# One kernel for two transformer blocks: the feed-forward stage's modulation columns computed in wide VectorE sums that TensorE adds up as rows of one PSUM bank

## The reference, cut to what matters

```python
# first block
mod = silu(c) @ w_ada[0] + b_ada[0]                  # 2048 -> 6 * 2048
shift1, scale1, gate1, shift2, scale2, gate2 = split(mod, 6)
h = modulate(rms(x, norm1_w), shift1, scale1)
...                                                   # state space mixer and attention
x = x + gate1 * mixed
h2 = modulate(rms(x, norm2_w), shift2, scale2)
ffn = (silu(h2 @ w_ffn_gate) * (h2 @ w_ffn_up)) @ w_ffn_down     # hidden width 5632
x = x + gate2 * ffn
# second block, layers 0 (attention, also over a context) and 1 (Fourier mixer)
sh_l, sc_l, g_l = split(silu(c_2) @ ada_w_2[i] + ada_b_2[i], 3)      # 2048 -> 3 * 2048
sh_c, sc_c, g_c = split(silu(c_ctx_2) @ ada_w_2[0] + ada_b_2[0], 3)  # layer 0, context
```

## Time and profile before

| | us |
|---|---|
| median of 3 runs | 2577.97 (2577.28 to 2579.29) |
| the profiled execution | 2578.01 |
| its span, first to last instruction | 2576.2 |

### The profile page before, as it was taken

The page is one execution under the profiler, slowest core; times in us unless marked ns, Lnnn a source line. Parts: engine busy times, 40 slices in busy tenths (PEclk is TensorE's granted clock), DMA queues, the critical chain, the costliest instruction groups (busy, mean ns, idle before and its releaser), DMA issues.

```text
span 2576.2 us, 38244 instructions
## 1 busy us (share of the span) xinstructions
PE 2443.4 (95%) x15542; PEld 2074.0 (81%) x15542; DVE 1653.1 (64%) x2005; ACT 1036.8 (40%) x1378; POOL 216.3 (8%) x193
## 2 busy tenths in 40 slices
PE   5899989989999999999999999999969999999995
PEld 1588766579888889898887888888758999999894
DVE  8655645457777777875776566455774584764547
ACT  2454764234333333333433454444423333333431
POOL 0139700020000000000011000000002000000000
PEclk9899999999999999999999999999989999999998
DMA  9854479958999999996453753333545585765551
GB/s 386 311 160 159 132 280 391 402 187 328 342 339 346 355 348 372 341 330 238 149 172 122 237 151 116 101 101 122 191 128 181 180 294 171 240 209 172 161 167 41
DMA packets 278064, 589.47 MB, mean 229 GB/s; under 512 B 20608, under 2 KB 29824, under 8 KB 276608
## 3 DMA queue, kind: packets, MB, share of 16 engines
q1 hardware_dynamic: 277888, 587.02, 66.3%
HBM read 584.85 MB, written 2.10 MB: 228 GB/s over the span
## 4 chain that ended last, share of the span: by engine, by line
PE 89%; DVE 5%; DMA 3%; ACT 2%; issue 1%; POOL 0%; SPq 0%; DVEq 0%; ACTq 0%
PE psum L206 13%; PE psum L208 12%; PE psum L207 12%; PE psum L218 12%; PE psum L219 12%; PE psum L220 12%; PE psum L278 3%; DMA start_slots<-in_w_ada 2%; PE psum L2435 1%; PE psum L1823 1%; DMA kt<-in_w_ada 1%; DVE wlo L195 1%; PE psum L426 1%; PE psum L2411 1%; PE psum L366 1%
## 5 line engine op out<-in xcount | busy, mean ns | idle before, releaser
L195 DVE TENSOR_TENSOR wlo<-raw,whi 128x1024 fp32r<-128x1024 f32 (+2 forms) x728 | 879.3, 1224 | 582.0 <-ACT whi L189 580.4
L189 ACT CAST whi<-raw 128x1024 fp32r<-128x1024 f32 (+2 forms) x728 | 736.8, 1022 | 961.7 <-PE psum L208 452.6
L218 PE MATMUL psum<-hh,whi 128*128 128x256 f32 x2688 | 760.8, 283 | 4.9 <-DVE wlo L195 4.4
L219 PE MATMUL psum<-hh,wlo 128*128 128x256 f32 x2688 | 750.8, 279 | 0.0
L220 PE MATMUL psum<-hl,whi 128*128 128x256 f32 x2688 | 750.8, 279 | 0.0
L218 PEld LDWEIGHTS psum<-hh,whi 128*128 128x128 f32 x2688 | 508.0, 189 | 28.1 <-issue 25.9
L220 PEld LDWEIGHTS psum<-hl,whi 128*128 128x128 f32 x2688 | 511.0, 190 | 0.0
L219 PEld LDWEIGHTS psum<-hh,wlo 128*128 128x128 f32 x2688 | 507.3, 189 | 1.6 <-issue 1.0
L206 PE MATMUL psum<-whi,hh 128*128 128x512 f32 (+1 forms) x736 | 298.6, 406 | 9.9 <-DVE wlo L195 6.7
L208 PE MATMUL psum<-whi,hl 128*128 128x512 f32 (+1 forms) x736 | 288.4, 392 | 0.0
L207 PE MATMUL psum<-wlo,hh 128*128 128x512 f32 (+1 forms) x736 | 287.1, 390 | 0.0
(11 more groups left out here) (353 smaller groups left out, 2253.6 us busy)
## 6 DMA issues: line engine op xcount, KB each, us to landing
araw<-in_ada_w SPq DMA_DIRECT2D x128, 512.0 KB, 6.4
raw<-in_w_in_fourier SPq DMA_DIRECT2D x128, 512.0 KB, 3.8
raw<-in_w_ffn_gate SPq DMA_DIRECT2D x88, 512.0 KB, 10.7
raw<-in_w_ffn_up SPq DMA_DIRECT2D x88, 512.0 KB, 7.7
raw<-in_w_ffn_down SPq DMA_DIRECT2D x88, 512.0 KB, 11.1
raw<-in_w_in_attn SPq DMA_DIRECT2D x88, 512.0 KB, 4.5
araw<-in_w_ada SPq DMA_DIRECT2D x80, 512.0 KB, 7.6
start_slots<-in_w_ada SPq DMA_DIRECT2D x64, 512.0 KB, 8.4
```

The lines of the kernel that those rows point to most:

```text
L189: nc.scalar.copy(whi[:, u % SPLITS, 0:kn, 0:w], raw[:, u % RING, 0:kn, 0:w]).then_inc(s_hi, 1)
L195: nc.vector.tensor_tensor(wlo[:, u % SPLITS, 0:kn, 0:w], raw[:, u % RING, 0:kn, 0:w], whi[:, u % SPLITS, 0:kn, 0:w].bitcast(F32), ALU.subt ...
L218: nc.tensor.matmul(o, h, hh[:, kt + k], start=(kt + k == 0 and f % 2 == 0), stop=False)
L219: nc.tensor.matmul(o, lw, hh[:, kt + k], start=False, stop=False)
```

## The change

It rewrites how the modulation is done beside the feed-forward steps 1 to 8.

- `ada_load` and `ada_sum` take a whole pair at once: loads are 128 rows by 1024 columns (still 512 KB), sums are 1024 wide, 16 for a pair. Places in the lists stay: two loads and two sums where there were two loads and four sums. Semaphores `ada_slot_landed` 0 to 3 and 4 to 7 change owners.
- For these eight pairs PE no longer makes columns. `row_sum` adds the partitions up as a row of bank 7, the bank of the rounds: 4 matmuls with a window of `ones_window` as 32 weight columns, on 256 columns each, in the four column groups, behind unit 19. `ada_store` is left out there. In the Fourier stage the reduction to columns and the store stay.
- Pair 15, which both condition vectors use, leaves the rounds. 3 rounds a step stay, behind units 5, 11 and 17. Its 16 row blocks are loaded in SP's places behind units 20 and 23 (`dual_load`) and summed by DVE, with both vectors, behind units 18 and 20 (`dual_sum`) into `acc2`, which lies where `lng` will be. PE adds both up as rows 16 and 17 behind the last unit of step 8 (`dual_reduce`).
- Set 3 then has 18 rows. `set_turn_pe` takes 18 columns of `select`, which is 32 wide now; `set_store_dve` makes six small additions for two. In step 9, copy, turn and store stand one unit later.
- `select` moves from behind `cond_windows` to behind `skip_columns`, with `ones_window` and a `spare` of 64 bytes. The buffers from `powers` on start 64 bytes lower, those behind the new ones 512 bytes higher.

```diff
-    sel = sb(ctx, "select", [P, 2, 8])
...
+    sel = sb(ctx, "select", [P, 2, 32])
+    onez = sb(ctx, "ones_window", [P, 64])
+    spare = sb(ctx, "spare", [P, 16])
...
-    PE_PAIRS = (0, 1, 2, 3, 4, 5, 6, 7, 8, 9, 12, 13, 14, 15)
-    PE_SETS = ((0, 4, 1), (4, 2, 1), (6, 4, 1), (10, 4, 2))
+    PE_PAIRS = (0, 1, 2, 3, 4, 5, 6, 7, 8, 9, 12, 13, 14)
+    PE_SETS = ((0, 4, 1), (4, 2, 1), (6, 4, 1), (10, 3, 2))
...
+            elif m >= 160:
+                step, k = divmod(m - 160, 6)
+                if k < 2:
+                    if step:
+                        sp.wait_ge(s_aused, R_FFN + 3 * step)
+                elif k < 4:
+                    if step:
+                        sp.wait_ge(s_dual, 2 * step - 3 + k - 1)
+                else:
+                    sp.wait_ge(s_aused, R_FFN + 3 * step + 1)
...
+        if n < 4:
+            sp.wait_ge(s_aused, set_rounds(2))
+        else:
+            sp.wait_ge(s_acc, n - 3)
+        sp.dma_start(arawf[:, 1024 * (kt % 4):1024 * (kt % 4) + 1024],
+                     w[kt * P:(kt + 1) * P, c:c + 2 * CW]).then_inc(s_slot[kt % 4], 16)
...
+    def row_sum(pe, a, row, stop=False):
+
+        for half in range(2):
+            for e in range(2):
+                g, cs = 2 * half + e, slice(2 * P * e, 2 * P * e + 2 * P)
+                ins = nc.tensor.matmul(psum[32 * g:32 * g + 32, 7, cs], onez[:, 31 - row:63 - row],
+                                       a[:, half * CW + 2 * P * e:half * CW + 2 * P * e + 2 * P], start=False, stop=stop,
+                                       tile_position=(0, 32 * g))
+        return ins
...
+    def ada_reduce(pe, q):
+
+        g = pair_rank(q)
+        pe.wait_ge(s_acc, 16 * (g + 1))
+        if g < 8:
+            row_sum(pe, acc, 8 + g).then_inc(s_red, 1)
+            return
...
+    def dual_load(sp, kt):
+
+        t, landed, _ = ffn_slot(kt // 2, 6 + kt % 2)
+        sp.wait_ge(s_aused, R_FFN + 3 * (kt // 2) + 2)
+        sp.dma_start(t, dram["ada_w_2"][0][kt * P:(kt + 1) * P, 3 * 1024:4 * 1024]).then_inc(landed, 16)
+
+    def dual_sum(dve, kt):
+        w, landed, count = ffn_slot(kt // 2, 6 + kt % 2)
+        dve.wait_ge(landed, count)
+        if kt:
+            dve.wait_ge(s_dual, kt)
+        for v in range(2):
+            s = cond[:, 16 + 16 * v + kt:17 + 16 * v + kt]
+            if kt == 0:
+                ins = nc.vector.tensor_scalar(acc2[:, v], w, s, None, ALU.mult)
             else:
...
+                ins = nc.vector.scalar_tensor_tensor(out=acc2[:, v], in0=w, scalar=s, in1=acc2[:, v],
+                                                     op0=ALU.mult, op1=ALU.add)
+        ins.then_inc(s_dual, 1)
+
+    def dual_reduce(pe):
+        pe.wait_ge(s_dual, 16)
+        row_sum(pe, acc2[:, 0], 16)
+        row_sum(pe, acc2[:, 1], 17, True).then_inc(s_dred, 1)
...
+            if not H.fourier and not first and c <= 8 and j in (18, 20):
+                dual_sum(dve, 2 * (c - 1) + (j - 18) // 2)
         if H.fourier and first:
             hidden_up_dve(dve, H, 0)
-        if q is not None:
+        if q is not None and H.fourier:
             ada_store(dve, q)
...
-            if not H.fourier and 1 <= c <= 8 and j % 6 == 5:
-                r = 80 + 4 * (c - 1) + j // 6
+            if not H.fourier and 1 <= c <= 8 and j in (5, 11, 17):
+                r = R_FFN + 3 * (c - 1) + j // 6
                 rounds_pe(pe, r, r + 1)
...
-            if q is not None and j == (13 if first else 19):
+            if q is not None and j == 19:
                 ada_reduce(pe, q)
+            if not H.fourier and c == 8 and j == 23:
+                dual_reduce(pe)
```

More of the change, by code:

```diff
@@ L272, in rounds_pe @@
             for e in range(2):
-                _, landed, count, _ = slot(2 * r + e)
+                _, landed, count = slot(2 * r + e)
                 pe.wait_ge(landed, count)
@@ L297, in set_turn_pe @@
             pe.wait_ge(s_mcol, st)
-        np_, vectors = PE_SETS[st][1:]
-        n = 4 * (vectors - 1) + np_
+        np_ = PE_SETS[st][1]
+        n = 18 if st == 3 else np_
         o = psum[:, 7, 0:8 * n].rearrange("p (r c) -> p c r", c=8)
@@ L312, in set_store_dve, with pair_rank @@
         if vectors == 2:
-            nc.vector.tensor_tensor(modx[:], psum[:, 7, n:2 * n], bias, ALU.add)
+            b0 = COLS["bada"].start
+            for o, row, k in ((modx[:, 0:n], 4, c0), (modx[:, 24:32], 17, 120), (modc[:, 80:96], 8, 80),
+                              (modc[:, 128:176], 10, 128), (modc[:, 120:128], 16, 120)):
+                w = o.shape[1]
+                nc.vector.tensor_tensor(o, psum[:, 7, 8 * row:8 * row + w], cols[:, b0 + k:b0 + k + w], ALU.add)
         nc.vector.tensor_tensor(modc[:, c0:c0 + n], psum[:, 7, 0:n], bias, ALU.add).then_inc(s_mcol, 1)
-    def dve_rank(q):
-        return q - 20 if q < 24 else q - 28
+    def pair_rank(q):
+        return (q - 20) // 2 if q < 24 else (q - 28) // 2
     def ada_src(q):
@@ L340, in program @@
[L340 to L365, removed]
-                ins = nc.tensor.matmul(psum[:, 6, 4 * c + j:4 * c + j + 1], acc[:, c, j * P:(j + 1) * P], ones[:, 0:1],
-                                       start=True, stop=True)
-        ins.then_inc(s_red, 2)
-    def ada_store(dve, q):
-        dve.wait_ge(s_red, dve_rank(q) + 2)
-        bias = cols[:, COLS["bada"].start + 4 * q:COLS["bada"].start + 4 * q + 8]
-        nc.vector.tensor_tensor(modc[:, 4 * q:4 * q + 8], psum[:, 6, 0:8], bias, ALU.add).then_inc(s_mod, 2)
+        return w, c * CW
@@ new lines, in ada_load, with ada_sum @@
+    def ada_load(sp, q, kt):
+        w, c = ada_src(q)
+        n = 16 * pair_rank(q) + kt
+        if n < 4:
[4 more added lines that the diff above has]
+                     w[kt * P:(kt + 1) * P, c:c + 2 * CW]).then_inc(s_slot[kt % 4], 16)
+    acc = powers[:].rearrange("p a b -> p (a b)")
+    def ada_sum(dve, q, kt):
+        g = pair_rank(q)
+        if kt == 0 and g:
+            dve.wait_ge(s_red, g)
+        dve.wait_ge(s_slot[kt % 4], 16 * (SLOT_USES[1] + 4 * g + kt // 4 + 1))
+        c0 = 0 if q < 24 else 16
+        w, s = arawf[:, 1024 * (kt % 4):1024 * (kt % 4) + 1024], cond[:, c0 + kt:c0 + kt + 1]
+        if kt == 0:
+            ins = nc.vector.tensor_scalar(acc, w, s, None, ALU.mult)
+        else:
+            dve.wait_ge(s_acc, 16 * g + kt)
+            ins = nc.vector.scalar_tensor_tensor(out=acc, in0=w, scalar=s, in1=acc, op0=ALU.mult, op1=ALU.add)
+        ins.then_inc(s_acc, 1)
@@ new lines, in row_sum @@
+    def row_sum(pe, a, row, stop=False):
[7 more added lines that the diff above has]
+    def ada_reduce(pe, q):
+        g = pair_rank(q)
+        pe.wait_ge(s_acc, 16 * (g + 1))
+        if g < 8:
+            row_sum(pe, acc, 8 + g).then_inc(s_red, 1)
+            return
+        if g > 8:
+            pe.wait_ge(s_mod, g - 8)
+        for j in range(8):
+            ins = nc.tensor.matmul(psum[:, 6, j:j + 1], acc[:, j * P:(j + 1) * P], ones[:, 0:1], start=True, stop=True)
+        ins.then_inc(s_red, 1)
@@ L1756, in hidden_dve @@
                 first_turn_dve(dve, H, j, j + 1)
-            pos = ADA24 if n == 24 else ADA_AFTER
-            if q is not None and j in pos:
-                a = pos.index(j)
-                ada_sum(dve, q + a // 4, a % 4)
+            if q is not None and j in ADA24:
+                for kt in range(2 * ADA24.index(j), 2 * ADA24.index(j) + 2):
+                    ada_sum(dve, q, kt)
+            if not H.fourier and not first and c <= 8 and j in (18, 20):
+                dual_sum(dve, 2 * (c - 1) + (j - 18) // 2)
         if H.fourier and first:
             hidden_up_dve(dve, H, 0)
-        if q is not None:
+        if q is not None and H.fourier:
             ada_store(dve, q)
```

81 lines of the change are left out of this document (44 added, 37 removed).

## The result

| | before | after |
|---|---|---|
| median of 5 runs, us | 2577.97 (2577.28 to 2580.12) | 2589.98 (2586.53 to 2592.20) |
| the profiled execution, us | 2578.01 | 2586.53 |
| its span, us | 2576.2 | 2584.7 |

The change makes the kernel slower by 12.0 us: 1.0043 times the time of before, 95% interval 1.0029 to 1.0058. The forecast was 2561.4 us and its range ended at 2573. The profiled execution of after is the fastest of its five, and its span is 8.5 us longer than that of before, so its rows show less than the whole loss.

A forecast was written before the change was run, and what follows sets the result against it. PE was taken to bound the kernel, so microseconds off its list count. Savings of 17.8 us less 1.2 us added gave 16.6, other terms 0: 2578.0 - 16.6 = 2561.4 us, range 2552 to 2573.

The forecast's parts named there:

- What bounds the kernel: In the eight feed-forward steps PE is busy 586.00 of 586.00 us; each microsecond taken from its list shortens the step.
- the part on what happens once: Outside the repeated steps: memsets, set 3's turn, Fourier sums, shifted buffers; 0, at most 0.5 us, except through the pace.
- Rival 1: Without unit 23's round, 256-column matmuls in steps 1 to 6 turn slow: 9.8 us back, 2571.2 us, chance 0.18.
- The terms on PE: Per step: one round less (1.19 us), column reduction gone (1.79), row sum added (0.76); `dual_reduce` once adds 1.19.
- Row sum: Four 256-column matmuls behind unit 19 in each step cost PE 0.76 us, bounds 0.43 and 1.19 us.
- rival 3: The row sum behind unit 19 costs a whole round, 1.19 us: saving 11.9 us, time 2566.1 us, chance 0.08.
- The whole sum of 16.6 us: PE's savings over eight steps, 17.8 us, less 1.2 us added at the end of step 8: net 16.6 us.
- the size of a sum: On DVE, one sum on 128x1024 takes 1.29 us, between 1.22 and 1.50.
- the wait: DVE waits 1.3 us at `dual_sum` behind unit 18; its lead falls to 3.4 us, costing PE 0.
- Rival 4: Two-vector loads hold up DVE and PE starves at `low` 19: 36.8 us lost, 2598 us, chance 0.05.
- The transfers: SP's loads keep places and sizes; 25 MB in a 71 us step asks for about 355 GB/s, cost 0.
- Rival 5: PE's list gets shorter but the step stays, because transfers then set it: 2578 us, chance 0.04.

The follow-up runs named there:

- e1: After with the 64-byte `spare` moved ahead of `powers`, so buffers from `powers` to `skip_columns` have the addresses of before: 2562.90 us.
- e2: Before with only `select` moved behind `skip_columns`, so buffers from `powers` to `skip_columns` start 64 bytes lower: 2607.51 us.
- e8: e1 with 96 bytes more ahead of the late buffers, so `hidh` starts 64 above a multiple of 128: 2543.52 us.
- e3: After with a `gap` of 128 bytes ahead of `powers`, which moves `hh` and also `hidh`: 2589.09 us.
- e9: e8 with 64 bytes ahead of `raw`, so every buffer from there on starts 64 higher and all distances stay: 2543.03 us.
- e6: After with the 64 bytes of `spare` between `hh` and `hl`, so `hh` stays low and `hl` lies as in before: 2587.89 us.
- e10: e8 with 256 bytes more ahead of `powers`, between `whi` and `hh`: 2542.78 us.
- e11: Before with a `gap` of 608 bytes behind `skip_columns`, so the late buffers lie as in e8: 2556.22 us.

## Why the prediction was wrong

**What bounds the kernel: right.** PE is the one resource that counts. In after and e1 it has no idle time in the eight steps, and each of its microseconds is one of the step.

**The step that failed** is the last sentence of the part on what happens once: "The buffers behind `cond_windows` start 64 bytes lower and the late ones 512 higher; same operations, 0, except by way of the pace". It was sized at nothing. It is a term of 29.1 us (e2 less before) or 27.1 us (after less e1), the largest of the whole sum and larger than the gain. The move by 64 bytes is the part that costs: it took `hh` from the distance 192 to 128. The 512 bytes of the late buffers left theirs as it was.

**Rival 1 had the right sign at the wrong size, by the wrong cause.** It saw that the pace of the 256-column matmuls could move, and even which view would show it. But it tied the move to the round that goes behind unit 23, priced it in six steps and with the slow level of before: 9.8 us. E1 has no such round and runs at 116.1 ns, within 0.6 of before; e2 has it and is slow. What the rival describes can be seen in e1, in a small size: in steps 2 and 4 to 7 units 0 to 6 are at the slow pace and those behind are mostly at the fast one. PE's timeline of e1, first matmuls of units 1, 2, 7 and 8 of step 2:

```profile
676.11 0.28 PE L220 MATMUL psum<-hh,whi 128*128 128x256 f32 x1
...
678.94 0.28 PE L220 MATMUL psum<-hh,whi 128*128 128x256 f32 x1
...
694.17 0.28 PE L220 MATMUL psum<-hh,whi 128*128 128x256 f32 x1
...
696.89 0.28 PE L220 MATMUL psum<-hh,whi 128*128 128x256 f32 x1
```

The first two are 2.83 us apart, the last two 2.72. In all it is 0.6 ns by 4224 matmuls, 2.5 us of the 9.8. That the missing round causes it isn't shown: e8 lacks the round too, and its steps 2, 3, 7 and 8 begin at the fast pace. In after, the pace moved in three stages of the kernel, to a level above before's slow one, and the matmuls with `hh` as weights, which were in no rival, lost 3 ns each. The prediction also took the pace to be one of whole steps. That holds for steps 1 to 8 of before but for the units behind a round; in steps 9 and 10 and in the Fourier stage it changes within a step. The two levels in one trace were a warning that spacings depend on something that isn't in the instruction. I took them for the whole range; they were only the range at one distance.

**The terms on PE: right.** They can be read in e1 and in after. Row sum: the timeline of after around it, behind unit 19 of step 3:

```profile
808.75 0.40 PE L210 MATMUL psum<-whi,hidl 128*128 128x512 f32 x1
809.08 0.64 PE L382 MATMUL psum<-powers,ones_window 128*32 128x256 f32 x8
809.65 0.50 PE L208 MATMUL psum<-whi,hidh 128*128 128x512 f32 x1
809.99 0.39 PE L209 MATMUL psum<-wlo,hidh 128*128 128x512 f32 x1
```

809.99 - 808.75 = 1.24 us, less two spacings of 0.234: 0.77 us, where 0.76 was forecast. That answers rival 3: had the fixed part around a change of shape been charged in full, it would be 1.19. The rule of the Trainium skill ("TensorEngine Tiling (Array Packing)", Key Properties) isn't contradicted: some 0.33 us of the 0.77 are more than the streaming. But they are no more than around a round. `dual_reduce`, in e1's timeline:

```profile
1172.21 0.40 PE L210 MATMUL psum<-whi,hidl 128*128 128x512 f32 x1
1172.53 1.07 PE L382 MATMUL psum<-lng,ones_window 128*32 128x256 f32 x16
1173.54 0.38 PE L220 MATMUL psum<-hh,whi 128*128 128x256 f32 x1
1173.76 0.28 PE L221 MATMUL psum<-hh,wlo 128*128 128x256 f32 x1
```

1.55 us, less one spacing of 0.23 and one of 0.12: 1.20 us, forecast 1.19. The one step at the fast pace takes 70.37 us (forecast 70.4). The whole sum of 16.6 us stands within some 1 us: 15.5 measured at the old place, with 2.5 us lost in e1 by the units at the slow pace (above) and 0.6 won in the Fourier stage (3072 x 0.2 ns), so the instructions themselves are worth some 17.4.

**DVE: the size of a sum right, the wait wrong in the harmless direction.** The groups by form of e1, 620 to 1160 us; busy us, mean ns of one, then the idle time before them:

```profile
L374 DVE SCALAR_TENSOR_TENSOR powers<-araw,cond,powers 128x1024 f32<-128x1024 f32 x113 | 144.9, 1282 | 6.3
L423 DVE SCALAR_TENSOR_TENSOR lng<-ffn_slots,cond,lng 128x1024 f32<-128x1024 f32 x30 | 37.2, 1280 | 0.3 <-DMA ffn_slots<-in_ada_w 0.3
```

1.28 us for 1.29. But the wait of 1.3 us in each step is 0.3 us in all. Its base, a landing after 12.0 us, was the median of two issues; in e1 the eight loads in the first of these two places land 9.4 to 10.9 us after their issue. SP is held up for less time in issuing it, 0.34 us where the earlier trace rows have 1.23. SP's queue and DVE's timeline of e1, step 3, then PE's first matmul of unit 19:

```profile
780.64 0.34 SPq L411 DMA_DIRECT2D ffn_slots<-in_ada_w  x1
```

```profile
790.42 1.23 DVE L197 TENSOR_TENSOR wlo<-raw,whi 128x1024 fp32r<-128x1024 f32 x1 [1.60 <-ACT whi L191]
791.57 2.48 DVE L423 SCALAR_TENSOR_TENSOR lng<-ffn_slots,cond,lng 128x1024 f32<-128x1024 f32 x2
793.96 1.22 DVE L1735 TENSOR_TENSOR hid<-sgb,psum 128x1024 f32<-128x1024 f32 x1
795.09 2.36 DVE L197 TENSOR_TENSOR wlo<-raw,whi 128x1024 fp32r<-128x1024 f32 x2
```

```profile
801.53 0.39 PE L208 MATMUL psum<-whi,hidh 128*128 128x512 f32 x1
```

`low` 19 is the first of DVE's last two and ends at 795.09 + 1.22 = 796.31. PE begins with unit 19 at 801.53, so the lead is 5.2 us, where 3.4 were forecast. Rival 4 needed it gone, and it never came near.

**The transfers: right.** A step of 71 us was to ask for about 355 GB/s; e1 moves 360 in its step of 70.37 us and 355 in that of 71.02, and PE waits for none of it. Rival 5 is out.

## What to carry to other kernels

When a change moves a buffer that TensorE reads, its address is part of the change: keep the old place with a pad, or price the move by a run of the old code with the new layout. A kernel that TensorE bounds is worth a comparison of start-to-start spacings by kind of matmul, at equal clock; a few ns between two traces of the same instruction, times some thousand, can be larger than what the edit was for. And where one trace shows two paces of one instruction and nothing that selects them, the range has to allow for a third.

## What the runs showed of the hardware

**The spacing of these rounded float32 matmuls with a new weight tile each depends on where `hh` and `hidh` lie relative to `whi`, modulo 256 bytes.** In the feed-forward stage, at a granted clock of 1.00, matmuls on 256 moving columns run at 115.5 to 116.1 ns for the distance 192, at 118.8 to 119.8 for 64, 128, 160 and 224, and at 121.0 for 0. With 512 moving columns the order is another one: 228.6 ns at 0, 229.2 to 229.5 at 192, 232.5 to 232.6 at 128, 233.3 to 233.4 at 64, 160 and 224, 234.1 to 234.3 at 96. (Part of the stretch before the feed-forward stage has a clock of 0.95 to 1.00, in before and after nearly alike; in the one from 400 to 540 us, at 1.00, the matmuls with `hh` as weights stand at 229.7 and 232.5 ns.)

Taken unit by unit, the place goes with whether the fast pace occurs at all in that stage. In the seven kernels with `hh` at 192, 81 to 105 of the 176 units of 256-column matmuls in the feed-forward stage are at 113 to 114 ns and all others at 117 or more; in the seven with another distance none of the 176 is below 117.

Shown is that for starts at multiples of 64 bytes the distance counts and not `hh`'s own address (before and e2, e3 and e9), and that with `hh` at a slow one `hl` at the fast one doesn't help (e6). For 96, 160 and 224 the distance can't be told from a start 32 bytes off a multiple of 64. Nor is it shown from which buffer to count: `raw`, `whi`, `wlo`, `araw` and `cond_windows` keep their distances from one another in all kernels, and `whi` is named because it is the other operand. That the two operands' reads get in each other's way is a reading of it, not shown: no view here shows a read of TensorE.

The Trainium skill ("TensorE: Matmul & The Clock Gate", "Step-by-step: what each phase is for") says that TensorE reads weights and moving data by two separate ports, so that loading the next weights takes no read bandwidth from the running matmul. It says nothing there of the place of the two. Before and e2 have the same instructions and are 29.1 us apart, so the place counts here; whether the ports have to do with it, no run shows. The Trainium skill ("SBUF — State Buffer", "Operand start alignment") asks for a start at a multiple of the element size and says of itself that it is about legality and timed nothing; every place here keeps to that, and the code of the change takes from 2542.78 to 2589.98 us by place alone.

**What stays open.** At the distance 192 the 256-column matmuls still have two paces, 113 and 118 ns, and what selects between them isn't known. In the Fourier stage, with `hidh` at 96 or 224, the distance of `hh` does little between 192 (117.7 to 118.5 ns), 64 and 160 (118.7 each); 128 and 0 are slower (119.9 to 121.2). There the fast pace came with the late buffers: e1 has mostly 118 ns, e8 mostly 113 from 1973 us on. E8 moved the other late buffers with `hidh`, so that gain can't be put down to one of them. Distances of 32 and 96 for `hh`, `hl` at another distance with `hh` at 192, a place of `wlo` apart from `whi`, and a move of all buffers by 32 bytes, which would settle the question of the alignment, weren't tried.

The fastest kernel of the study is e10, equal to e8 and e9 within the measurement: 2542.78 us, 1.4% under before, of which the change's code has some 13 (e11 less e10) to 16 us (before less e1) and the place the other 20 or so.
